# A decoder layer on eight cores: the start of the kernel rearranged, and three reorderings in its second pass

## The chip, the cores and the metric

One Trainium2 chip, eight cores, each with TensorE (PE in the profile), VectorE (DVE), ScalarE (ACT), GpSimd (POOL) and the queue engine SyncE (SP). Every core runs the same program on its own prompt sequence of 2048 rows and its own 16 sample rows, with the same weights. No core waits for another. The metric is the device time of the slowest core in microseconds.

## The reference, cut to what matters

```python
def layer(h, p, prev_a, prev_ffn, ...):
    xn = rmsnorm(h, g_mix)
    z = xn @ w_in                      # 1024 x 7168: x_a, b_a, c_a, u|v, g_a, g_b
    a_conv, new_a = causal_dwconv(c_a * x_a, w_conv_a, prev_a)
    y_a = (b_a * a_conv) @ w_out_a
    u, v = split(gelu(uv)); v = rmsnorm(v, g_v)
    s = chunk_spatial(v, w_spatial, b_spatial)
    y_b = (u * s) @ w_out_b
    m = sigmoid(ga) * y_a + sigmoid(gb) * y_b
    h = h + m @ w_o
    up = rmsnorm(h, g_ffn) @ w_up      # 1024 x 5632
    up_c, new_ffn = causal_dwconv(up, w_conv_ffn, prev_ffn)
    h = h + (gelu(fa) * fb) @ w_down   # 2816 x 1024
    gate = sigmoid(rmsnorm(h, g_ple) @ w_ple_gate)
    return h + gate * (p @ w_ple), ...
```

All inputs and outputs are float32 in memory. The layer runs once for the prompt and once for the sample rows, with a last rmsnorm on both. The weights are used by both groups.

## The kernel before, in words

The 2048 prompt rows go through the layer in two passes of 1024 rows (`pss` 0 and 1), eight tiles of 128 rows each. The 16 sample rows ride along in the second pass (`samp`), as columns 1024 to 1039 of the transposed activations. All products are bfloat16 with sums in PSUM, which has eight banks of 512 float32 columns.

*Order of work.* Every operation is recorded in one list for each engine, in the order of the Python program. `P.op` and `P.dma` derive the semaphore waits from the names that an operation reads and writes, such as `("h", t)` for a tile of rows or `("ps", b)` for a PSUM bank. An engine works through its list strictly in order. So an instruction that waits holds up all behind it on its engine, SP's and POOL's DMA issues among them.

*Weights.* They are packed in memory in the order of their use. `Ring` loads them through POOL's queue, which also casts them to bfloat16, into a ring of eight slots. An item of 512 columns (`w512`) takes two slots and 2 MB of float32, one of 256 columns a slot and 1 MB. `R.limit` caps how many items may have been issued. It is 1 at first (the first value weights, item 0), 2 after the square of row tile 5 (the second value weights, item 1), and open behind the last square.

*The head.* SP issues the loads of the row tiles h0 and h1, then h2 when h0 is there, h3 when item 0 is there, h4 when h1 and item 0 are there, and h5, h6, h7 when h2, h3, h4 are there. A `TileNorm` then takes ACT for the sum of squares, POOL for the inverse root, DVE for the scaling into bfloat16 (L510), PE for eight transposes (L326), and DVE for the copy out of PSUM with the gain (L335). The loop over t runs the value product `B_mm(0, 0, t)` (eight matmuls of 512 columns, L322), `heads[t + 3].scale()` and `heads[t + 2].tp()`. The second half `B_mm(0, 1, t)` needs item 1. PSUM banks 0 to 5 go round among the products, 6 and 7 among the transposes.

*The stages of a pass.* Value product and short conv with its products x, c, b; the spatial gating with the matrix `WsT` and for the sample rows `Ds`, made by `setup_spatial` at j = 4 of the first pass; merge; output product with `w_o` into bank pairs `2 * (t % 3)`, after which DVE adds to h; up product and conv, with `cp` over 11 pairs of weight items; down product; per-layer embedding. In the first `cp` the list `order` says in which order half products ("a" and "b", of blocks q), transposes of the last two row tiles ("T6", "T7"), sample products ("S0", "S1") and the conv of a pair ("E0", "E1") are issued. In the second pass the up products use three bank pairs in rotation, from pair 0, and the transposes and sample products banks 6 and 7. In the down product, four row tiles at a time (`grp`) sum over three weight items (`q`). The sample rows' share `pHs`, in bank 2, follows the four tiles of `grp` 1 after each item.

Of the kernel before, what the change touches and what calls it, by code (L numbers as in the profile page):

```python
# [10 lines left out]
ALU = mybir.AluOpType  # L11
# [3 lines left out]
NS = 16  # L15
# [185 lines left out]
def build_program():  # L201
# [24 lines left out]
    with es:  # L226
# [107 lines left out]
        def TTT(eng, out, in0, in1, op, reads, writes):  # L334
            P.op(eng, lambda e: e.tensor_tensor(out=out, in0=in0, in1=in1, op=op), reads=reads, writes=writes)  # L335
# [20 lines left out]
        class Ring:  # L356
# [8 lines left out]
            def _try_load(self):  # L365
                i = self.next_load
                if i >= NIT or i >= self.limit:
                    return False
                kind, w, k0, nk, c0 = all_items[i]
                ns = 2 if kind == "w512" else 1  # L370
                s = self.slot_ptr
                if ns == 2 and s % 2 == 1:
                    s = (s + 1) % 8
                for q in range(ns):
                    occ = self.occupant[(s + q) % 8]
                    if occ is not None and occ not in self.released:
                        return False
                width = ITEM_W[kind]
                flat = ring[:, s:s + ns, :].rearrange("p a b -> p (a b)")
                land = flat[:, 0:nk * width]  # L380
                dst = land.rearrange("p (k n) -> p k n", k=nk)
                o = ITEM_OFF[i % len(ITEMS)]
                wsrc = wpk_d[o:o + 128 * nk * width].rearrange("(p l) -> p l", p=128)
                res = [("ring", (s + q) % 8) for q in range(ns)]
                P.dma("pool", (lambda e: e.dma_start(out=land, in_=wsrc)), f"wr{s}", writes=res)  # L385
                for q in range(ns):
                    self.occupant[(s + q) % 8] = i
                self.item_slot[i] = (dst, res)
                self.slot_ptr = (s + ns) % 8
                self.next_load += 1  # L390
                return True
# [37 lines left out]
        P.op("pool", lambda e: e.memset(epsc[:, 0:1], EPS), writes=["epsc"])  # L429
        P.op("pool", lambda e: e.memset(epsc[:, 1:2], 4.0 * EPS), writes=["epsc"])  # L430
        R.prefetch()
        v0r = R.item_slot[0][1]
        for t, after in ((2, [("h", 0)]), (3, v0r), (4, [("h", 1)] + v0r), (5, [("h", 2)]), (6, [("h", 3)]), (7, [("h", 4)])):
            load_h(0, t, after)
        P.op("pool", lambda e: e.memset(ones[:], 1.0 / 1024.0), writes=["ones"])
        P.op("pool", lambda e: e.memset(carry_a[:], 0.0), writes=[("carry_a", j) for j in range(8)])
# [19 lines left out]

        def setup_spatial(stg):
            (ws, wsr), (tr, trr) = stg
            TTT("dve", WsT[:], ws[:, 0:1024].rearrange("p (j t) -> p j t", j=8), bc_mid(tr[:, 0:128], 8), ALU.mult, [wsr, trr], ["WsT"])
            for j in range(8):  # L460
                P.op("dve", lambda e, j=j: e.tensor_scalar_mul(out=Ds[:, j, :], in0=idf[0:16, 0:16], scalar1=w00[0:16, j:j + 1]),
                     reads=["cst"], writes=["Ds"])
            wideR.free(wsr)
            wideR.free(trr)
# [151 lines left out]
        for t in range(8):  # L616
            jk, jkr = wideR.get()
            heads.append(TileNorm(h[:, t, :], ("h", t), 128, t * 128, t, 0, dma=False, junk=(jk[:, 0:512].bitcast(BF16), jkr)))
            heads[t].sq()
            if t == 5:  # L620
                R.limit = 2
                R.prefetch()
        R.limit = NIT
        R.prefetch()
        heads[0].scale()
        heads[1].scale()
        heads[0].tp()
        heads[1].tp()
        heads[2].scale()
        for t in range(8):  # L630
            B_mm(0, 0, t)
# [10 lines left out]
        for pss in range(2):  # L642
# [128 lines left out]
                hsf = hs[:].rearrange("p k s -> p (k s)")  # L771
            for t in range(8):
                mres = [("m", k, bi) for bi, (c0, n) in enumerate(blocks) if c0 < (t + 1) * 128 and c0 + n > t * 128 for k in range(8)]
                pO, pOr = psR.at(2 * (t % 3), 2)
                for half in range(2):
                    _, wv_, wvr = wo[half]
                    for k in range(8):
# [74 lines left out]
            for cp in range(11):  # L852
# [1 line left out]
                ib_, wb, wbr = next_item()  # L854
                pairs = {}
                if cp == 0 and samp:
                    order = [(0, "a", 0), "T6", (0, "b", 0), (1, "a", 0), "T7", "S0", "S1", (0, "a", 1), (0, "b", 1), "E0",
                             (1, "a", 1), (1, "b", 0), (1, "b", 1), "E1"]
                elif cp == 0:
                    order = [(0, "a", 0), "T6", (0, "b", 0), (1, "a", 0), "T7", (1, "b", 0), (0, "a", 1), (0, "b", 1), "E0",  # L860
                             (1, "a", 1), (1, "b", 1), "E1"]
                else:
                    order = [(0, "a", 0), (0, "a", 1), (0, "b", 0), (0, "b", 1), "E0", (1, "a", 0), (1, "a", 1), (1, "b", 0), (1, "b", 1), "E1"]
                    if samp:
                        order[5:5] = ["S0"]
                        order.append("S1")
# [43 lines left out]
            if samp:  # L910
                store(cf_d[:, :], carry_f[:].rearrange("p r c -> p (r c)"), "stcf", [("carry_f", c) for c in range(44)])
                store(cfs_d[:, :], sfT[:].rearrange("p s r c -> p (s r c)"), "stcfs", ["sfT"] + [("sfTo", c) for c in range(44)])
            for half in range(2):
                its = [next_item() for _ in range(3)]
                hc = slice(half * 512, (half + 1) * 512)
                for grp in range(2):
# [3 lines left out]
                    for q in range(3):  # L920
                        _, wv_, wvr = its[q]
                        lo, hi = q * 8, min(22, q * 8 + 8)
                        for tt in range(4):
                            t = grp * 4 + tt
                            pp, ppr = bk[tt]
                            for c in range(lo, hi):
                                MM(pp, act[:, c, t * 128:(t + 1) * 128], wv_[:, c - lo, :], c == 0, c == 21,
                                   wvr + [("act", c)], ppr + (["R1busy"] if c == 21 else []), c == hi - 1)
                            if q == 2:
                                STT(h[:, t, hc], pp, 2.0, h[:, t, hc], ALU.mult, ALU.add, ppr + [("h", t)], [("h", t)])  # L930
                                if half == 1:
                                    pipe.push(TileNorm(h[:, t, :], ("h", t), 128, t * 128, t, 2))
                        if samp and grp == 1:
                            for i in range(4):
                                for c in range(lo, hi):
                                    MM(pHs[:, i * NS:(i + 1) * NS], wv_[:, c - lo, i * 128:(i + 1) * 128], act[:, c, 1024:1040],
                                       i == 0 and c == 0, i == 3 and c == 21, wvr + [("act", "s")],
                                       pHsr + (["R1busy"] if c == 21 else []), c == hi - 1)
                            if q == 2:
                                hh = hsf[:, half * 64:(half + 1) * 64]  # L940
                                STT(hh, pHs[:, 0:64], 2.0, hh, ALU.mult, ALU.add, pHsr + ["hs"], ["hs"])
                        if pss == 0 and half == 0:
                            if (grp, q) == (0, 2):
                                sqp = sample_sq()
# [233 lines left out]
```

How the kernel before makes its waits and increments, by code:

```python
            def body(engine, ops=ops):  # L157
                for fn, waits, sig in ops:
                    for k, v in waits:
                        engine.wait_ge(sems[k], v)
                    if fn is None:
                        continue
                    ins = fn(engine)
                    if sig is not None:
                        if sig[0] == "eng":
                            ins.then_inc(sems[sig[1]], 1)
                        else:
                            ins.then_inc(sems[sig[1]], 16)
```

## Time and profile before

| | us |
|---|---|
| median of three runs | 1170.34 (1170.22 to 1171.02) |
| profiled execution, its own time | 1170.05 |
| its span on the slowest core (core 2) | 1168.3 |
| spans of the eight cores | 1163.5 to 1168.3 |
| PE busy (core 2) | 1124.1 (96%) |
| DVE, ACT, POOL busy | 609.8, 384.7, 341.8 |
| chain that ended last, share of PE | 88% |

The span is the time from the first to the last instruction of a core; the profiled execution's own time is 1.75 us longer. All rows below are of core 2 unless they say otherwise. Times in them are microseconds from the start of the span. The granted clock is 1.00 for the higher of PE's two levels. The five DMAs of rows 4 were issued at 1.85 (V0, item 0), 7.6 (h2), 16.4 (h3), 24.4 (h7) and 28.1 (V1, item 1).

### The profile page before, as it was taken

The numbers are of one execution on the slowest core, as the hardware profiler recorded it, in microseconds if no ns is written. First come the engines' busy times: TensorE is split into PE (matmuls) and PEld (weight loads), VectorE is DVE, ScalarE is ACT, GpSimd is POOL, SyncE is SP. The second block draws the span as 40 slices with busy tenths as digits, with TensorE's granted clock in tenths as the row PEclk, the third lists the DMA queues.
The fourth block names the chain that finished last, engine by engine and source line by source line (L and its number), as shares of the span: only waits on it lengthen the run. The fifth ranks groups of instructions, "written<-read, shape, count | busy, mean of one in ns | idle before, by whom it ended". The sixth has DMA issues, their size and how long they took to land.

```text
span 1168.3 us, 18289 instructions; the slowest of 8 cores (1163.5 to 1168.3 us)
## 1 busy us (share of the span) xinstructions
PE 1124.1 (96%) x6425; PEld 574.5 (49%) x6520; DVE 609.8 (52%) x668; ACT 384.7 (33%) x649; POOL 341.8 (29%) x451
## 2 busy tenths in 40 slices
PE   4999999999999999999899999999999999999996
PEld 2444454444444444443446666666644444444443
DVE  3267662123687776124615866322267888871247
ACT  3622221111354444014772223112133444430134
POOL 2411113222234434114832010222223333330144
PEclk9999999999999999999999999999999999999998
DMA  7983642544844333358699355244377343343443
GB/s 185 183 158 72 111 71 46 80 83 78 145 93 72 73 73 72 62 92 192 196 195 233 63 116 90 37 73 73 72 127 127 73 73 73 73 90 64 79 102 129
DMA packets 58585, 119.77 MB, mean 103 GB/s; under 512 B 33264, under 2 KB 34032, under 8 KB 55936
## 3 DMA queue, kind: packets, MB, share of 16 engines
q0 software_dynamic: 20112, 82.85, 40.9%
q1 hardware_dynamic: 38240, 35.58, 11.3%
q8 instruction: 54, 0.88, 0.3%
q14 instruction: 35, 0.29, 0.1%
q10 hardware_dynamic: 144, 0.17, 0.1%
HBM read 184.14 MB, written 9.95 MB: 166 GB/s over the span
## 4 chain that ended last, share of the span: by engine, by line
PE 88%; POOL 3%; issue 2%; DVE 2%; DMA 2%; ACT 1%; DVEq 0%; POOLq 0%; ACTq 0%; SPq 0%
PE pq L322 88%; POOL s_wd L335 2%; DMA s_ring<-wpk 1%; DVE s_wd L338 1%; ACT s_xnb L329 1%; POOL s_st_r L335 1%; POOL s_st_ss L335 1%; DMA s_h<-x 1%; ACT s_wd L329 0%; DVE s_h L338 0%; PE pq L326 0%; POOL s_R L335 0%; DVE s_xnb L510 0%; DVE s_xnb L338 0%; DVE s_xn L335 0%
## 5 line engine op out<-in xcount | busy, mean ns | idle before, releaser
L322 PE MATMUL pq<-s_xn,s_ring 128*128 128x512 bf16 (+3 forms) x3693 | 658.1, 334 | 4.2 <-DVE s_wd L338 0.8
L322 PEld LDWEIGHTS pq<-s_xn,s_ring 128*128 128x128 bf16 x3744 | 335.6, 98 | 313.2 <-issue 2.0
L338 DVE SCALAR_TENSOR_TENSOR s_wd<-pq,s_cst,s_wd 128x1023 f32<-128x1023 f32 (+1 forms) x176 | 225.2, 1282 | 63.1 <-ACT s_carry_f L332 53.8
L335 POOL TENSOR_TENSOR s_R<-s_wd 128x1024 bf16<-128x1024 f32 (+3 forms) x84 | 146.3, 1742 | 357.9 <-DVE s_wd L338 166.6
L322 PE MATMUL pq<-s_ring,s_R 128*128 128x512 bf16 x936 | 206.9, 379 | 2.7 <-DVE s_wd L338 1.4
L338 DVE SCALAR_TENSOR_TENSOR s_wd<-s_wd,pq 128x512 f32<-128x512 f32 (+4 forms) x98 | 66.7, 681 | 193.2 <-PE pq L322 170.4
L329 ACT ACTIVATE s_wd<-pq 128x512 f32<-128x512 f32 (+4 forms) x138 | 78.4, 568 | 240.1 <-PE pq L322 238.7
L329 ACT ACTIVATE s_wd<-pq,s_cst 128x1024 f32<-128x1024 f32 x88 | 98.1, 1114 | 165.5 <-PE pq L322 165.5
L322 PEld LDWEIGHTS pq<-s_ring,s_R 128*128 128x128 bf16 x960 | 93.2, 98 | 112.5 <-issue 1.8
L322 PE MATMUL pq<-s_R,s_ring 128*128 128x347 bf16 (+3 forms) x875 | 125.1, 292 | 0.3
L322 PE MATMUL pq<-s_ring,s_xn 128*128 128x512 bf16 (+1 forms) x514 | 119.6, 383 | 5.3 <-DMA s_ring<-wpk 3.3
L385 POOL DMA_DIRECT2D s_ring<-wpk x134 | 75.0, 564 | 132.7 <-PE pq L322 127.5
L322 PEld LDWEIGHTS pq<-s_R,s_ring 128*128 128x128 bf16 x880 | 69.7, 97 | 50.9
L329 ACT ACTIVATE s_xnb<-s_h 128x1024 bf16<-128x1024 f32 x32 | 33.8, 1057 | 184.8 <-DVE s_h L338 184.4
L322 PEld LDWEIGHTS pq<-s_ring,s_xn 128*128 128x128 bf16 (+1 forms) x528 | 50.4, 98 | 65.2 <-issue 9.8
L335 POOL TENSOR_TENSOR s_st_ss<-s_st_ss,s_epsc 128x1 f32<-128x1 f32 (+1 forms) x81 | 24.3, 300 | 160.3 <-ACT s_xnb L329 139.7
L338 DVE SCALAR_TENSOR_TENSOR s_h<-pq,s_h 128x512 f32<-128x512 f32 x32 | 22.1, 690 | 93.3 <-PE pq L322 93.3
L335 DVE TENSOR_TENSOR s_wd<-pq,s_wd 128x512 f32<-128x512 f32 (+2 forms) x40 | 23.5, 587 | 70.7 <-POOL s_wd L342 26.7
L338 DVE SCALAR_TENSOR_TENSOR s_wd<-s_wd,s_cst 128x1024 f32<-128x1024 f32 x32 | 41.1, 1285 | 24.1 <-ACT s_wd L329 22.5
L335 POOL TENSOR_TENSOR s_st_r<-s_st_ss,s_mhalf 128x1 f32<-128x1 f32 (+1 forms) x81 | 47.3, 584 | 12.0 <-POOL s_st_ss L335 0.9
L329 ACT ACTIVATE s_wd<-s_wd 128x1024 f32<-128x1024 f32 (+1 forms) x45 | 47.3, 1056 | 5.1 <-DVE s_wd L335 5.1
L338 DVE SCALAR_TENSOR_TENSOR s_xnb<-s_h,s_st_r,s_gbc 128x1024 bf16<-128x1024 f32 x28 | 35.9, 1282 | 11.1 <-POOL s_st_r L335 8.5
(81 smaller groups left out, 483.6 us busy)
## 6 DMA issues: line engine op xcount, KB each, us to landing
s_ring<-wpk POOLq DMA_DIRECT2D x110, 512.0 KB, 8.9
s_ring<-wpk POOLq DMA_DIRECT2D x20, 1024.0 KB, 10.0
s_h<-x SPq DMA_DIRECT2D x16, 512.0 KB, 16.1
y<-s_wd SPq DMA_DIRECT2D x15, 512.0 KB, 2.7
s_R<-x SPq DMA_DIRECT2D x8, 512.0 KB, 9.2
s_ring<-wpk POOLq DMA_DIRECT2D x4, 768.0 KB, 7.2
s_gbc<-g_v SPq DMA_DIRECT2D x2, 512.0 KB, 15.0
s_gbc<-g_ffn SPq DMA_DIRECT2D x2, 512.0 KB, 6.3
```

The lines of the kernel that those rows point to most:

```text
L322: P.op("pe", lambda e: e.matmul(out, lhsT=lhsT, rhs=rhs, start=start, stop=stop), reads=reads, writes=writes, signal=signal)
L329: P.op("act", lambda e: e.activation(out=out, in_=in_, func=func, **kw), reads=reads, writes=writes)
L335: P.op(eng, lambda e: e.tensor_tensor(out=out, in0=in0, in1=in1, op=op), reads=reads, writes=writes)
L338: P.op("dve", lambda e: e.scalar_tensor_tensor(out=out, in0=in0, scalar=scalar, in1=in1, op0=op0, op1=op1), reads=reads, writes=writes)
L385: P.dma("pool", (lambda e: e.dma_start(out=land, in_=wsrc)), f"wr{s}", writes=res)
```

## The change

The head: item 0 is loaded by two DMAs, each with half of its columns in memory. The first writes the name `v0a`, the second the ring slots. The products of item 0 wait for both. h2 is released by `v0a`, h3 by h1 and `v0a`, and h4 to h7 by the tile two before each. `R.limit` becomes 2 after the square of tile 4 instead of 5. `warm(18)` and `warm(28)` put products of 128 columns, whose results nobody reads, behind the first and the second transpose, in bank 5. `setup_spatial` moves from DVE to POOL.

The second pass: the bank pairs of the output product start with pair 2. S1 moves behind E0 and the half product (1, "a", 1). The sample rows' share of the down product, now in `sample_H`, comes ahead of the four tiles for the last weight item and not behind them, and with it the update of `hs`.

```diff
@@ Ring._try_load
-                P.dma("pool", (lambda e: e.dma_start(out=land, in_=wsrc)), f"wr{s}", writes=res)
+                if i == 0:
+
+                    for q, wr in ((0, ["v0a"]), (1, res)):
+                        P.dma("pool", (lambda e, q=q: e.dma_start(out=land[:, q * 2048:(q + 1) * 2048], in_=wsrc[:, q * 2048:(q + 1) * 2048])),
+                              "wv0a" if q == 0 else f"wr{s}", writes=wr)
+                else:
+                    P.dma("pool", (lambda e: e.dma_start(out=land, in_=wsrc)), f"wr{s}", writes=res)
...
-                self.item_slot[i] = (dst, res)
+                self.item_slot[i] = (dst, res + ["v0a"] if i == 0 else res)
@@ head
-        v0r = R.item_slot[0][1]
-        for t, after in ((2, [("h", 0)]), (3, v0r), (4, [("h", 1)] + v0r), (5, [("h", 2)]), (6, [("h", 3)]), (7, [("h", 4)])):
+        for t, after in ((2, ["v0a"]), (3, [("h", 1), "v0a"]), (4, [("h", 2)]), (5, [("h", 3)]), (6, [("h", 4)]), (7, [("h", 5)])):
             load_h(0, t, after)
@@ setup_spatial
-            TTT("dve", WsT[:], ws[:, 0:1024].rearrange("p (j t) -> p j t", j=8), bc_mid(tr[:, 0:128], 8), ALU.mult, [wsr, trr], ["WsT"])
+            TTT("pool", WsT[:], ws[:, 0:1024].rearrange("p (j t) -> p j t", j=8), bc_mid(tr[:, 0:128], 8), ALU.mult, [wsr, trr], ["WsT"])
             for j in range(8):
-                P.op("dve", lambda e, j=j: e.tensor_scalar_mul(out=Ds[:, j, :], in0=idf[0:16, 0:16], scalar1=w00[0:16, j:j + 1]),
+                P.op("pool", lambda e, j=j: e.tensor_scalar_mul(out=Ds[:, j, :], in0=idf[0:16, 0:16], scalar1=w00[0:16, j:j + 1]),
@@ head
-            if t == 5:
+            if t == 4:
                 R.limit = 2
                 R.prefetch()
...
+        def warm(n):
+            pw, pwr = psR.at(5)
+            for q in range(n):
+                MM(pw[:, 0:128], ones[:], idb[:], True, True, ["ones", "idb"], pwr, q == n - 1)
+
         heads[0].tp()
+        warm(18)
         heads[1].tp()
+        warm(28)
@@ output product
-                pO, pOr = psR.at(2 * (t % 3), 2)
+                pO, pOr = psR.at(2 * ((t + (2 if samp else 0)) % 3), 2)
@@ up product
-                    order = [(0, "a", 0), "T6", (0, "b", 0), (1, "a", 0), "T7", "S0", "S1", (0, "a", 1), (0, "b", 1), "E0",
-                             (1, "a", 1), (1, "b", 0), (1, "b", 1), "E1"]
+                    order = [(0, "a", 0), "T6", (0, "b", 0), (1, "a", 0), "T7", "S0", (0, "a", 1), (0, "b", 1), "E0",
+                             (1, "a", 1), "S1", (1, "b", 0), (1, "b", 1), "E1"]
@@ down product
+            def sample_H(pHs, pHsr, wv_, wvr, lo, hi, half):
+                for i in range(4):
+                    for c in range(lo, hi):
+                        MM(pHs[:, i * NS:(i + 1) * NS], wv_[:, c - lo, i * 128:(i + 1) * 128], act[:, c, 1024:1040],
+                           i == 0 and c == 0, i == 3 and c == 21, wvr + [("act", "s")],
+                           pHsr + (["R1busy"] if c == 21 else []), c == hi - 1)
+                if hi == 22:
+                    hh = hsf[:, half * 64:(half + 1) * 64]
+                    STT(hh, pHs[:, 0:64], 2.0, hh, ALU.mult, ALU.add, pHsr + ["hs"], ["hs"])
...
+                        if samp and grp == 1 and q == 2:
+                            sample_H(pHs, pHsr, wv_, wvr, lo, hi, half)
                         for tt in range(4):
...
+                        if samp and grp == 1 and q < 2:
+                            sample_H(pHs, pHsr, wv_, wvr, lo, hi, half)
```

## Rows read from the trace of the kernel before

**Rows 1.** Spans and granted clock of all cores.

```profile
core 1: 1163.5 us, clock 0.998
```

**Rows 2.** PE's waits over the span: total, times, longest (us).

```profile
PE pq L326 <- DVE s_xnb L510: 13.6, 5, 10.8
```

**Rows 3.** Timeline of the head: start, length, engine, line, operation, count, idle before.

```profile
16.57 3.57 PE L322 MATMUL pq<-s_ring,s_xn 128*128 128x512 bf16 x8 [3.12 <-DMA s_ring<-wpk]
...
20.21 1.01 PE L326 MATMUL pq<-s_idb,s_xnb 128*128 128x128 bf16 x8
...
24.39 1.06 ACT L329 ACTIVATE s_wd<-s_h 128x1024 bf16<-128x1024 f32 x1 [1.95 <-DMA s_h<-x]
...
25.69 1.06 ACT L329 ACTIVATE s_wd<-s_h 128x1024 bf16<-128x1024 f32 x1
...
28.12 0.59 POOL L385 DMA_DIRECT2D s_ring<-wpk  x1
...
28.71 1.89 PE L322 MATMUL pq<-s_ring,s_xn 128*128 128x512 bf16 x8 [0.53 <-DVE s_xn L335]
...
33.05 1.89 PE L322 MATMUL pq<-s_ring,s_xn 128*128 128x512 bf16 x7
...
39.05 6.20 PE L322 MATMUL pq<-s_ring,s_xn 128*128 128x512 bf16 x27 [0.18 <-DMA s_ring<-wpk]
```

**Rows 4.** DMA issues (V0, h2, h3, h7, V1), last column us to landing.

```profile
s_ring<-wpk POOLq DMA_DIRECT2D x1, 1024.0 KB, 14.5
...
s_h<-x SPq DMA_DIRECT2D x1, 512.0 KB, 9.4
...
s_h<-x SPq DMA_DIRECT2D x1, 512.0 KB, 4.8
...
s_h<-x SPq DMA_DIRECT2D x1, 512.0 KB, 5.1
...
s_ring<-wpk POOLq DMA_DIRECT2D x1, 1024.0 KB, 10.7
```

**Rows 5.** Timeline of core 1 at the end of the first half.

```profile
32.58 7.74 PE L322 MATMUL pq<-s_ring,s_xn 128*128 128x512 bf16 x35
```

**Rows 6.** Stretches of the head: busy by engine, PE clock, DMA share, GB/s.

```profile
9.00:11.00 2.00, 0.16 (x2) 0.19 (x3) 0.75 (x1) 0.97 (x2) 1.43 (x4) 1.00 0.90 139
...
11.00:13.00 2.00, 1.41 (x14) 1.17 (x13) 1.46 (x2) 0.00 (x0) 0.43 (x1) 1.00 1.06 164
...
13.00:15.00 2.00, 0.45 (x5) 0.18 (x2) 1.65 (x2) 0.00 (x0) 0.00 (x0) 1.00 0.91 209
...
15.00:17.00 2.00, 0.43 (x2) 0.18 (x3) 0.00 (x0) 0.00 (x0) 0.00 (x0) 1.00 0.42 164
...
19.00:21.00 2.00, 1.93 (x11) 0.97 (x10) 0.75 (x1) 0.00 (x0) 0.21 (x1) 1.00 1.12 301
```

**Rows 7.** Timeline of DVE in the first conv stage.

```profile
110.01 1.22 DVE L335 TENSOR_TENSOR s_WsT<-s_wd 128x1024 bf16<-128x1024 f32 x1
```

**Rows 8.** Timeline of the second pass, output products to first up products.

```profile
844.82 6.85 PE L322 MATMUL pq<-s_ring,s_R 128*128 128x512 bf16 x31 [0.98 <-DVE s_wd L338]
...
874.04 1.89 PE L322 MATMUL pq<-s_xn,s_ring 128*128 128x512 bf16 x8
...
874.38 1.22 DVE L338 SCALAR_TENSOR_TENSOR s_h<-s_h,pq 128x1024 f32<-128x1024 f32 x1 [1.04 <-PE pq L322]
...
876.42 0.61 PE L326 MATMUL pq<-s_idb,s_xnb 128*128 128x128 bf16 x8 [0.48 <-DVE s_xnb L510]
...
888.54 11.79 PE L322 MATMUL pq<-s_xn,s_ring 128*128 128x512 bf16 x67 [0.80 <-DVE s_wd L338]
```

**Rows 9.** Timeline at the end of the second pass's down stage.

```profile
1118.62 0.75 PE L322 MATMUL pq<-s_R,s_ring 128*128 128x16 bf16 x24
...
1122.41 1.06 ACT L329 ACTIVATE s_xnb<-s_h 128x1024 bf16<-128x1024 f32 x1 [1.06 <-DVE s_h L338]
...
1124.15 1.02 PE L322 MATMUL pq<-s_ring,s_pT 128*128 128x512 bf16 x4 [1.31 <-DVE s_hs L338]
```

More of the change, by code:

```diff
@@ L932, in build_program @@
                                     pipe.push(TileNorm(h[:, t, :], ("h", t), 128, t * 128, t, 2))
[L933 to L941, printed above, removed]
+                        if samp and grp == 1 and q < 2:
+                            sample_H(pHs, pHsr, wv_, wvr, lo, hi, half)
                         if pss == 0 and half == 0:
```

## The prediction

> **What bounds the kernel now.** I first read the spans of all cores [rows 1]. The metric is the slowest core, core 2 with its 1168.3 us of the table above; the reader is to see that core 1 does the same work in 1163.5 us. The profiled execution took 1170.05 us, so 1.75 us lie outside its span, and it is 0.3 us under the median of 1170.34; I add all changes to the median. The table gives TensorE (PE) 1124.1 of 1168.3 us, so about 44 us are not PE, and only these, not the products, can be won by an edit that reorders. The waits of PE [rows 2] say where: the largest entry is the transposes of the head, which wait for scaled rows, 13.6 us in five times, one of them 10.8 us, which is the wait for the first row tile itself. So the second view is the timeline of the first 40 us [rows 3]. Call the eight row tiles of pass 0 h0 to h7, the two loads of value weights V0 and V1, and the eight products of each value half B0 to B7. B0 starts at 16.57, when V0 has landed; B3 at 28.71; B5 at 33.05; the second half starts at 39.05, and from there PE runs without a long gap. The head is therefore worth 39.05 minus 16 products, whatever PE could do.
>
> Three rows tell what B3 waited for. The square of h4 starts at 24.39, when h4 has landed, and B3 starts 4.3 us later. The code says why it is h4 and not h3: the scaling of h(t+1) stands on VectorE (DVE) ahead of the copy that B(t) reads. The transpose of h2 starts at 20.21, and h2 landed at 7.6 + 9.4 = 17.0 [rows 4], 3.2 us before. From B3 on the step is (33.05 - 28.71) / 2 = 2.17 us, PE's own (eight products, eight transposes), and from B5 to the second half it is 6.0 us, of which 0.2 is a wait for V1. So on core 2 three things end within a fifth of a microsecond: the chain h4, B3, four steps; and V1, issued at 28.12 with 10.7 us to landing. Core 1 shows the same program when neither is late [rows 5]: its B6 starts at 32.58 and runs on into the second half without a gap, so that half starts at 36.05. Core 2 is 3.0 us later there, two thirds of the distance of the spans. A head that only helps core 1 is worth nothing to the metric.
>
> **The head, step by step.** (1) *V0 in halves.* The products still name both halves, so B0 starts no sooner by it; the first half is only the token that releases h2 and h3. When does it land? From 9 to 17 us the queues moved 2 x (139 + 164 + 209 + 164) = 1352 thousand bytes [rows 6]; h2 is 524 of them, so V0 took 828 and had 221 of its 1049 before 9.0. Half of V0 is 524, 303 more, and the 139 GB/s of the first row are V0 nearly alone: 2.2 us, so about 11.2. Bounds: 10.3 if the half is served ahead of the tail of h1, 12.5 with one more microsecond of completion. The cost of the second issue on POOL (GpSimd) is one more DMA instruction before two memsets that nobody waits for: nothing.
>
> (2) *h2 and h3.* Before, h2 was issued at 7.6 and took 9.4 us, against 4.8 for h3 [rows 4]: it landed behind V0. Now it is issued at 11.3. The bytes ahead of it are the same and the queues stay busy, so I take 17.0 again; the lower bound is 11.3 + 4.8 = 16.1, the upper one 18. h3 is issued with it and not at 16.4. Four tiles from h3 (21.2) to h7 (24.4 + 5.1 = 29.5) took 8.3 us, 2.1 each, so h3 lands at 19.1 instead of 21.2.
>
> (3) *h4 to h7.* Each is now released by the tile two before it. At 4.8 us a load: h4 17.1 + 4.8 = 21.9, h5 24.0, h6 26.8, and h7 24.1 + 5.1 = 29.2. The new list keeps two loads under way and no more, so the gain shrinks: 2.4 us at h4, 0.3 at h7.
>
> (4) *Fillers.* 18 and 28 products of 128 columns stand behind the two first transposes. B0 took 3.57 us for eight products, 0.45 each, where B3's row shows 1.89: 512 columns in 0.43 us are the lower of the clock's two levels, 1.2 GHz, though the clock column of [rows 6] reads 1.00 there; PE had been idle for 3.12 us. With the fillers it is busy up to V0, and I expect B0 at the higher level, 1.7 us shorter. But the next instruction is the transpose of h2, and that cannot start before 17.0 + 3.2 = 20.2, where it starts now. So the 1.7 us become a wait: worth nothing, unless h2 is sooner. Their cost: 46 products at half of a transposed block's time or so (8 take 1.01 us at the lower level in the row of the transpose) end by about 17.5 at most, up to 0.9 us after V0; hidden by the same wait.
>
> (5) *The chain.* B2 not before 19.1 + 4.3 = 23.4; B3 21.9 + 4.3 = 26.2; B4 28.4 (B3 plus 2.17; h5 gives 28.3); B5 26.8 + 4.3 = 31.1; B6 29.2 + 4.3 = 33.5, and two products follow, so the half starts at 31.1 + 5.8 = 36.9 to 37.1. Against 39.05 that is 2.1 us. (6) *V1 a tile sooner.* Before, the issue at 28.12 came 2.4 us after the square of h5 had started at 25.69 [rows 3]; now it follows h4: 21.9 + 2.4 = 24.3, landing 24.3 + 10.7 = 35.0, inside the 37.0. It buys nothing of itself, but without it V1 would land at 24.0 + 2.4 + 10.7 = 37.1 and set the end. Bounds of the head: 1.0 us gained if h2 is at 18; 4.4 if loads overlap better (rival one). (7) *The spatial setup on POOL.* DVE loses one operation of 1.22 us [rows 7] and eight of 16 columns; PE has no wait there on core 2, so nothing. POOL gets them, at up to twice DVE's time as my guess (no row here shows it); behind them on POOL stand 2-column copies and weight loads. A load that comes some 4 us later costs nothing as long as PE has no wait for the ring there, and it has none behind the head: nothing too.
>
> **The second pass.** (8) *PSUM banks.* Now the first output product goes to banks 0 and 1, and bank 0 is the last one of the merge: PE waits 0.98 us for DVE (the first of [rows 8]). With the banks rotated it goes to 4 and 5, whose readers are done: 0.95 saved. But the eighth tile then lies in banks 0 and 1, and that is where the first up product is written. DVE reads that tile from 874.38 for 1.22 us, to 875.60. The product starts at 874.04 today; it would start at about 875.75, end 1.72 later at 877.5, and the transpose behind it, which starts at 876.42 today after 0.48 us of waiting, starts 1.1 to 1.3 later. So the rotation gives 0.95 and takes 1.2: plus 0.25 us. Between the bounds 0 (if the wait is hidden in what follows) and 1.66.
>
> (9) *S1 later.* Today both sample products stand before the up product that needs the second transposed tile and waits for its copy anyway; moved, S1 (16 products of 16 columns, 0.5 us by the 0.75 of 24 in [rows 9]) falls into the 0.80 us in front of 888.54. It is hidden before and after: 0, at most 0.1 either way. (10) *Sample product of the down stage first.* At the end of the stage PE waits 1.31 us for DVE's update of the sample rows, in bank 2 [rows 9]. Moved ahead of the last four tiles, the update is done early and this wait goes. What is late next: the sample norm's product behind it needs ScalarE (ACT), which first squares the last tile; that square starts at 1122.41, and the tile comes 0.75 us later than before, because the 24 sample products (0.75 us) now precede it. 1122.41 + 0.75 + 1.25 + 0.31 gives 1124.7, and with 0.15 to PE 1124.9, against 1125.0 today (1124.15 plus four products of 0.215). So 0.15 us are left of 1.31; bounds 0 and 1.3.
>
> **Sum.** Head -2.1, bank rotation +0.25, S1 0, sample product -0.15: -2.0 us, 1168.3.
>
> **Rivals.** *One: the head follows bandwidth, not the two loads.* If a tile lands every 1.75 us (524 thousand bytes at the 301 GB/s of the one stretch of [rows 6] that is h loads alone), with h2 at 16.5, h7 is there at 25.5 and PE's own step decides: transposes of h2 at 19.7 (0.45 us), then five steps of 2.17 us and two of 1.72, the half at about 34.5, V1 just there: -4.4, total 1165.9, and 1164.8 if the sample wait goes too. Against it: h3 alone took 4.8 us. The same sum holds for a bank wait that is hidden. *Two, the other side: V1 breaks into h7.* V1 issued at 24.3 moves its first data at about 27 (an estimate: h3's 4.8 us less 1.75 of its own transfer leave 3 us at most), when h7 (issued 24.1) is half done. h2 next to V0 took 4.6 us more than h3. If h7 suffers as h2 did it lands at 29.2 + 4.6 = 33.8, B6 starts at 38.1, and the half at 41.6: +2.5, total 1173. It decides from 2 us of delay of h7 on. For it: h2's row. Against it: h7 is under way first, and V0 was under way before h2. The Trainium skill, "DMA: Bandwidth & Descriptors", section "Queues, rings and completion order", says that an engine takes turns between queues by whole packets of several descriptors and not row by row; by that h2 waited for V0's packet, which agrees with its 9.4 us, and h7, already begun, would lose nothing to V1, so that the sum stays at -2.0 rather than +2.5. *Three: the first half of V0 lands only with the second,* because both go through one queue at the same time. Then h2 is issued at 16.4 and lands at 21.2, h3 at 23.3, h4 at 26.1, h6 at 31.0: B5 35.3, the half at 41.1: +2.0, total 1172.4. Against it: the order of issue.
>
> **From cases to numbers.** About what a measurement of this kernel can tell from no change is 0.2%, 2.3 us; faster means below 1168.0. The forecast 0.55, its own range 1167.0 to 1169.6; it lies across that bound, 0.22 of it below. Rival one 0.23, all faster. Rival two 0.14, in its mild forms within the bound (0.06), else slower (0.08). Rival three 0.08: slower 0.05, within 0.03. So faster 0.45, same 0.42, slower 0.13. The range from 1165.3 to 1171.9 leaves out the far ends of all three.
>
> **What would show it.** Right: h2's transpose at about 20.2; the square of h4 near 22; V1's issue near 24; the second half at 37 on cores 0, 2, 5 and 7; B0 in 1.9 us with a wait behind it; no wait at the first output product, a new one of 1.7 us before the first up product; the wait for the sample update replaced by one for ACT. Wrong: h4 before 21 (rival one), h7 after 31 (rival two), h2 after 20 (rival three), a late stage that gives the head's gain back.

## The result: slower by 0.7%, because h7 waits for V1

| | before | after |
|---|---|---|
| median on the same chip, us | 1171.02 (5 runs) | 1178.95 (1176.71 to 1179.61, 5 runs) |
| ratio after / before | | 1.0068, 95% interval 1.0055 to 1.0080 |
| profiled execution, its own time | 1170.05 | 1176.71 |
| slowest core, its span | core 2, 1168.3 | core 1, 1174.5 |

The change costs 8 us where 2 were forecast as gain. One of the five executions of the kernel before (1258.06 us) was in the chip's slower state, in which the cores of a die show a lower granted clock; the ratios here and below leave such executions out. The first view is again the list of spans; it answers to [rows 1].

```profile
core 0: 1166.4 us, clock 0.996
core 1: 1174.5 us, clock 0.994
core 2: 1172.9 us, clock 0.993
core 3: 1165.2 us, clock 0.996
```

Six cores stand at 1172.9 to 1174.5 us, and two, 0 and 3, at 1166.4 and 1165.2. Something catches a core or misses it. The chain that ended last, on core 2 of the kernel after, names it (start, length, what):

```profile
1.84 9.59 DMA s_ring<-wpk
...
11.93 5.31 DMA s_h<-x
...
17.30 4.97 DMA s_h<-x
...
22.33 12.47 DMA s_h<-x
```

These are the first half of V0 (it lands at 11.43), then h3, h5 and h7, each issued when the one before in the chain has landed. h7 takes 12.47 us where h3 and h5 take 5. The timeline of core 2 of the kernel after (it answers to [rows 3]) has the rest:

```profile
15.04 1.89 PE L322 MATMUL pq<-s_ring,s_xn 128*128 128x512 bf16 x8 [0.85 <-DMA s_ring<-wpk]
19.27 1.01 PE L326 MATMUL pq<-s_idb,s_xnb 128*128 128x128 bf16 x8 [2.34 <-DVE s_xnb L515]
20.07 3.08 PE L322 MATMUL pq<-s_ring,s_xn 128*128 128x512 bf16 x8
...
21.73 1.02 POOL L391 DMA_DIRECT2D s_ring<-wpk  x1
...
34.88 1.06 ACT L329 ACTIVATE s_wd<-s_h 128x1024 bf16<-128x1024 f32 x1 [9.86 <-DMA s_h<-x]
...
38.23 1.01 PE L326 MATMUL pq<-s_idb,s_xnb 128*128 128x128 bf16 x8 [6.39 <-DVE s_xnb L515]
39.47 19.14 PE L322 MATMUL pq<-s_ring,s_xn 128*128 128x512 bf16 x80 [0.22 <-DVE s_xn L335]
58.44 3.83 PE L322 MATMUL pq<-s_xn,s_ring 128*128 128x512 bf16 x17
```

V1 is issued at 21.73 and h7 0.6 us behind it, at 22.3. The DMA issues of the two (the last column is the time to landing) and the stretches of the head answer to [rows 4] and [rows 6]:

```profile
s_ring<-wpk POOLq DMA_DIRECT2D x1, 1024.0 KB, 12.9
...
s_h<-x SPq DMA_DIRECT2D x1, 512.0 KB, 12.5
```

```profile
31.00:33.00 2.00, 0.85 (x4) 0.19 (x2) 0.00 (x0) 0.00 (x0) 0.00 (x0) 1.00 0.54 86
33.00:35.00 2.00, 0.00 (x0) 0.00 (x0) 0.00 (x0) 0.12 (x1) 0.00 (x0) 1.00 0.03 8
...
37.00:39.00 2.00, 0.77 (x8) 0.78 (x8) 1.78 (x2) 1.94 (x4) 2.00 (x5) 0.50 0.24 16
```

V1 lands at 21.73 + 12.9 = 34.6 and h7 at 34.8, right behind it. PE has finished B5 by 31.85, waits 6.39 us for the last scaled row, and then runs at the lower of its two clock levels for a while (0.50 granted in the row from 37 to 39 us): 80 matmuls of 512 columns take 19.14 us, where 80 x 0.215 is 17.2. The first product of the conv stage, the stage after the head, starts at 58.44; on core 2 before it was 52.86. Of these 5.6 us, 3.45 are the later transpose of h7 (38.23 against 34.78) and 2.1 come behind it, 1.9 of them from the clock. I use the start of the conv stage from here on as the mark of the head.

What the slowest cores differ by is (core 1 after against core 2 before): head 60.19 - 52.86 = +7.3; a wait at the end of pass 0 that core 1 does not have, -1.45 (below); second pass +0.3. Together +6.2, the difference of the spans.

The second pass, on core 1 of the kernel after, answers to [rows 8]:

```profile
849.51 7.07 PE L322 MATMUL pq<-s_ring,s_R 128*128 128x512 bf16 x32
...
879.29 1.22 DVE L338 SCALAR_TENSOR_TENSOR s_h<-s_h,pq 128x1024 f32<-128x1024 f32 x1 [1.04 <-PE pq L322]
...
880.66 1.89 PE L322 MATMUL pq<-s_xn,s_ring 128*128 128x512 bf16 x8 [1.54 <-DVE s_h L338]
882.39 0.61 PE L326 MATMUL pq<-s_idb,s_xnb 128*128 128x128 bf16 x8
```

The wait of 0.98 in front of the output products is gone, and one of 1.54 stands in front of the first up product, for the DVE operation on the eighth tile's banks.

### The profile page after: what moved, and what is told of

Read it like the earlier page. It is cut to its first block, busy times and chain, and to the rows that moved or that the text cites. A ratio compares the mean times of both kernels' runs of the same rounds, so it can differ in the third digit from the quotient of the medians.

```text
span 1174.5 us, 18478 instructions; the slowest of 8 cores (1165.2 to 1174.5 us)
## 1 busy us (share of the span) xinstructions
PE 1132.9 (96%) x6566; PEld 579.2 (49%) x6566; DVE 609.0 (52%) x659; ACT 384.5 (33%) x649; POOL 349.7 (30%) x461
## 4 chain that ended last, share of the span: by engine, by line
PE 90%; DMA 3%; POOL 3%; issue 2%; DVE 1%; ACT 1%; DVEq 0%; POOLq 0%; ACTq 0%; SPq 0%
PE pq L322 90%; DMA s_h<-x 2%; POOL s_wd L335 1%; DMA s_ring<-wpk 1%; DVE s_wd L338 1%; POOL s_st_ss L335 1%; POOL s_st_r L335 1%; ACT s_xnb L329 0%; PE pq L326 0%; DVE s_h L338 0%; ACT s_wd L329 0%; POOL s_rsS L335 0%; DVE s_xnb L515 0%; DVE s_xn L335 0%; DVEq L1129 0%
## 5 line engine op out<-in xcount | busy, mean ns | idle before, releaser
L338 DVE SCALAR_TENSOR_TENSOR s_wd<-pq,s_cst,s_wd 128x1023 f32<-128x1023 f32 (+1 forms) x176 | 225.1, 1282 | 63.6 <-ACT s_carry_f L332 53.5
L322 PE MATMUL pq<-s_R,s_ring 128*128 128x512 bf16 (+3 forms) x880 | 125.2, 292 | 0.0
L322 PEld LDWEIGHTS pq<-s_R,s_ring 128*128 128x128 bf16 x880 | 69.4, 97 | 50.4
L329 ACT ACTIVATE s_xnb<-s_h 128x1024 bf16<-128x1024 f32 x32 | 33.8, 1057 | 184.5 <-DVE s_h L338 184.1
L322 PEld LDWEIGHTS pq<-s_ring,s_xn 128*128 128x128 bf16 (+1 forms) x528 | 50.4, 98 | 61.7 <-issue 5.3
L335 POOL TENSOR_TENSOR s_st_ss<-s_st_ss,s_epsc 128x1 f32<-128x1 f32 (+1 forms) x81 | 23.9, 296 | 165.5 <-ACT s_xnb L329 138.0
L338 DVE SCALAR_TENSOR_TENSOR s_wd<-s_wd,s_cst 128x1024 f32<-128x1024 f32 x32 | 42.2, 1318 | 24.1 <-ACT s_wd L329 22.5
L338 DVE SCALAR_TENSOR_TENSOR s_xnb<-s_h,s_st_r,s_gbc 128x1024 bf16<-128x1024 f32 x28 | 35.9, 1282 | 11.2 <-POOL s_st_r L335 7.7
## 6 DMA issues: line engine op xcount, KB each, us to landing
s_h<-x SPq DMA_DIRECT2D x16, 512.0 KB, 17.3
```

The lines of the kernel that those rows point to most:

```text
L322: P.op("pe", lambda e: e.matmul(out, lhsT=lhsT, rhs=rhs, start=start, stop=stop), reads=reads, writes=writes, signal=signal)
L329: P.op("act", lambda e: e.activation(out=out, in_=in_, func=func, **kw), reads=reads, writes=writes)
L338: P.op("dve", lambda e: e.scalar_tensor_tensor(out=out, in0=in0, scalar=scalar, in1=in1, op0=op0, op1=op1), reads=reads, writes=writes)
```

## The experiments

The ratio is against the kernel before on the same chip. "Head" is the range over the eight cores of the start of the conv stage, "h7" that of its square; before they are 49.7 to 53.0 and 26.4 to 29.6, after 50.4 to 60.2 and 28.3 to 37.1.

| experiment | ratio, 95% interval | h7 | head |
|---|---|---|---|
| 1 after, V1 behind h5 again | 1.0018 [1.0009, 1.0027] | 27.6 to 30.6 | 50.8 to 53.2 |
| 2 before, V1 a tile sooner | 0.9994 [0.9985, 1.0003] | 27.6 to 30.6 | 50.3 to 53.5 |
| 3 after, h7 released by h4 | 1.0010 [1.0001, 1.0019] | 25.6 to 29.0 | 50.4 to 53.5 |
| 4 before, second pass of after | 0.9992 [0.9978, 1.0005] | 27.2 to 30.4 | 50.2 to 53.6 |
| 5 before, V1 two tiles sooner | 1.0036 [1.0021, 1.0051] | 27.1 to 32.2 | 50.0 to 54.5 |
| 6 experiment 1 without fillers | 1.0011 [0.9999, 1.0022] | 27.5 to 29.6 | 50.6 to 53.0 |
| 7 before, fillers alone | 1.0005 [0.9996, 1.0014] | 27.5 to 31.0 | 50.4 to 54.9 |
| 8 before, sample product alone | 0.9999 [0.9990, 1.0008] | 27.2 to 29.8 | 50.1 to 54.7 |
| 9 before, h7 released by h6 | 1.0037 [1.0025, 1.0050] | 29.1 to 35.2 | 50.9 to 59.3 |
| 10 after, V1 in two loads | 1.0054 [1.0035, 1.0074] | 27.1 to 38.5 | 49.3 to 62.7 |
| 11 head of 3, no fillers, second pass of before | 0.9987 [0.9975, 0.9999] | 26.8 to 28.4 | 50.2 to 52.0 |
| 12 before, banks alone | none, 1171.16 us once | 27.1 to 30.6 | 50.0 to 54.8 |

**1 and 2: V1's place, alone.** In the kernel after, `if t == 4:` becomes `if t == 5:`; in the kernel before, the reverse.

> The changed kernel, with the one edit that V1 is issued after the square of row tile 5 again. Theory A (V1 reaches the queues at the time of h7, and h7 lands behind it): h7 is back at 5 us from issue to landing on all cores, V1 is issued near 26 and lands near 37, the second half starts at 37 to 38 on the slow cores, and the time is 1168 to 1170 us, ratio 0.998 to 1.000. Theory B (the later release of h4 to h7, each by the tile two before it, costs by itself): h7 still lands after 31 and the time stays above 1175, ratio over 1.004. Theory C (the edits of the second pass cost several us): the head is cured, the time still above 1174.

> The kernel before, with V1 issued after the square of tile 4 instead of 5, and nothing else. In it h7 is released by h4's landing, 2.2 us ahead of V1's issue. Theory A: h7's data are under way first, it lands at 29.5 to 31 on most cores, V1 lands 1.5 to 2 us sooner; the time is 1168 to 1171, ratio 0.998 to 1.001, unless V1 catches h7 on some core, which then shows 10 us and more from issue to landing and about 1175. If issuing V1 a tile sooner is harmful in any order of release: ratio over 1.004.

Putting V1 back takes most of the loss away, though not all of it: the forecast for theory A was a ratio of 0.998 to 1.000, and 1.0018 came out. The rest is looked for below. But V1 sooner in the kernel before costs nothing: there h7 is released by h4 and goes out 2.1 to 2.5 us ahead of V1 on all eight cores. It takes both edits, the earlier V1 and the later h7.

**3: h7 ahead again, V1 early.** In the list of the kernel after:

```diff
-(4, [("h", 2)]), (5, [("h", 3)]), (6, [("h", 4)]), (7, [("h", 5)])
+(4, [("h", 1), "v0a"]), (5, [("h", 2)]), (6, [("h", 3)]), (7, [("h", 4)])
```

> The changed kernel, with the releases of h4 to h7 as before the change, one tile sooner each (h4 by h1 and the first half of V0, h5 by h2, h6 by h3, h7 by h4), V1 still after the square of tile 4. h7 is then issued 2.2 us ahead of V1. Theory A: h4 lands near 20.5, h7 near 27, V1 near 35, the second half starts at 35 to 36.5 on all cores, and the time is 1165 to 1168, ratio 0.995 to 0.998. Theory B says the same of the releases; the two differ in the run without the early V1. If V1 still catches h7: above 1174.

The square of h7 starts by 29.0 at the latest, with V1 left early: the other cure. The time was missed, 1.0010 where 0.995 to 0.998 was expected; the head starts its conv stage at 50.4 to 53.5, not sooner than before.

**5 and 9: the same fault from either side in the kernel before.** Experiment 5 has `if t == 3:`, experiment 9 `(7, [("h", 6)])` with V1 where it was.

> The kernel before with one edit: V1 issued after the square of h3, two tiles sooner (h7 still released by h4, V0 whole, no fillers, second pass unchanged). V1's issue should then stand within about 1 us of h7's on most cores. Theory (a load of h issued less than about 1 us before V1, or behind it, lands only when V1 has landed): the square of h7 moves from 26.4 to 29.6 us to 33 to 37 us on the cores where that happens, the first product of the stage after the head starts near 58 us there instead of 50 to 53, and the time rises by 4 to 8 us (ratio 1.003 to 1.007). Rival (what holds h7 back is two loads in flight and not V1; bandwidth is shared evenly): h7 lands by 31 us on all cores, ratio 0.999 to 1.001.

> The kernel before with one edit: h7 is released by h6 instead of h4. V1 keeps its place behind the square of h5 (issued at 24.6 to 28.2 us); h7 is issued at the landing of h6, 24.8 to 28.4 us, so within about 1 us of V1. Theory (the order of h7 against V1 decides, not that V1 is sooner): h7's square moves from 26.4 to 29.6 us to 35 to 39 us on several cores, where it lands with V1, the stage after the head starts 5 to 9 us later there, and the ratio is 1.003 to 1.008. Rival (an early V1 is harmful because h5 and h6 are still to come, h7's order is not the point): h7 lands 4 to 6 us after its issue, square at 30 to 33 us, stage after the head at most 3 us later, ratio 1.000 to 1.003.

Core 7 of experiment 9, timeline:

```profile
24.87 0.59 POOL L385 DMA_DIRECT2D s_ring<-wpk  x1
25.16 1.06 ACT L329 ACTIVATE s_wd<-s_h 128x1024 bf16<-128x1024 f32 x1 [1.54 <-DMA s_h<-x]
...
35.14 1.06 ACT L329 ACTIVATE s_wd<-s_h 128x1024 bf16<-128x1024 f32 x1 [8.83 <-DMA s_h<-x]
```

h6 lands at 25.1 and sends h7 out 0.3 us behind V1; h7 lands ten microseconds later. V1 was no sooner than in the kernel before, so the rival that blames an early V1 falls: the order of the two counts. This release also delays h7 by itself: on core 4, where it took only 5.6 us, its square starts at 34.1. So the times to landing carry this reading more than the ratio does.

The DMA queues of core 7, from 29 to 31 us and from 31 to 33 (packets, MB, share of the time of the 16 DMA engines), show what goes on meanwhile. q0 carries V1 in 128 packets of 8 KB, q1 carries h7 in 128 packets of 4 KB:

```profile
q0 software_dynamic: 41, 0.34, 80.0%
q1 hardware_dynamic: 44, 0.18, 23.6%
...
q0 software_dynamic: 38, 0.31, 90.5%
q1 hardware_dynamic: 37, 0.15, 20.8%
```

The two take turns, nearly one packet for one, which fits that both land together (34.9 and 35.1), and V1's packets take 80 to 90% of the engines' time. Not every core looks like this. On core 1 of the kernel after, between 26 and 30 us, q0 has 53 packets and q1 a single one, and nearly all of h7 (issued at 24.9) moves after 30. Why it starts so late there no run tells.

In the profiled execution of experiment 5 no core was caught fully (1171.94 us, h7's square by 32.2, where 33 to 37 was expected), but eight of its other eleven executions took 1176 to 1180 us, with single cores some 7 us above the rest. That h7 was caught on these cores is inferred from their times; they have no trace. Read together, the profiled executions of after and of 5, 9 and 10 give 32 cores with h7 from 1.3 us ahead of V1 to 1.6 behind:

| h7's issue against V1's | cores | h7, issue to landing |
|---|---|---|
| ahead by 0.05 to 1.3 us | 19 | 18 in 3.5 to 6.3 us, one 10.7 |
| behind by 0.1 to 1.6 us | 13 | 11 in 8.3 to 12.5 us, two in 5.7 and 7.0 |

In the ten other traces h7 is at least 2.1 us ahead on all 80 cores, and none takes more than 8.2 us.

**10: is it the size of the load?** V1 too goes out as two loads of 512 KB, one behind the other.

```diff
-if i == 0:
+if i < 2:
```

> The kernel after with V1 loaded as two transfers of 512 KB, one issued right behind the other, at the same place. Theory A (a load of h waits for the whole transfer that is ahead of it on the engines, one at a time): h7 is caught by the first half alone and lands 5 to 7 us after its issue; square at 28 to 31 us, ratio 1.001 to 1.003. Theory B (it waits for everything that the other queue has, both halves): h7's square at 33 to 37 us on most cores as in the kernel after, ratio 1.005 to 1.008.

The ratio is theory B's, but neither theory fits all cores. Four have h7 ahead of both halves and land it in 4.2 to 6.2 us. The other four, with h7's issue counted from that of V1's first half:

| core | h7 behind the first half | V1's halves land | h7 lands |
|---|---|---|---|
| 2, ahead of the second half | 0.8 | 32.3 and 36.5 | 32.5 |
| 6, ahead of the second half | 0.4 | 33.3 and 37.2 | 33.6 |
| 3, behind both | 1.3 | 34.8 and 37.5 | 37.3 |
| 5, behind both | 1.6 | 33.8 and 39.0 | 38.4 |

So h7 lands with the load that was issued last ahead of it: with the first half alone on cores 2 and 6, with the second on 3 and 5. That is theory A's rule, but not its size: the half alone still held h7 for 8.3 and 8.9 us, where 5 to 7 were expected.

**6 and 7: the fillers.** The two calls of `warm` are taken out of experiment 1, and put alone into the kernel before.

> The first experiment (the kernel after, V1 again behind the square of h5), and the two groups of filler products taken out. Its only difference from the first experiment, which stood at ratio 1.0018, is the 46 fillers. Theory (the fillers end before the transpose of h2 is due and the clock falls again where B0 waits, so they buy nothing): B0 takes 3.4 to 3.7 us instead of 1.9 and the start of the second half moves by less than 0.5 us, ratio 1.001 to 1.0025. Rival (the fillers pay for part of the head): ratio 1.003 or more, the second half 1 to 2 us later. A third way: they cost something, because the group of 28 holds up the transpose of h2; then ratio 1.000 to 1.001.

> The kernel before with the 18 and 28 filler products alone (V0 whole, the releases and V1 as before, second pass unchanged). Theory (fillers are worth nothing, h2 lands long after them): ratio 0.999 to 1.001, the start of the stage after the head stays at 49.7 to 53.0 us. Rival (full clock at B0 carries through the first half): 1 to 2 us faster, ratio 0.998 to 0.999.

Their worth is nothing that can be measured (1.0011 without them against 1.0018 with them, 1.0005 alone). Core 6 of experiment 6, timeline of PE, shows why the head doesn't gain in another way:

```profile
15.66 3.57 PE L322 MATMUL pq<-s_ring,s_xn 128*128 128x512 bf16 x8 [2.97 <-DMA s_ring<-wpk]
19.82 0.61 PE L326 MATMUL pq<-s_idb,s_xnb 128*128 128x128 bf16 x8 [0.58 <-DVE s_xnb L515]
...
36.77 13.97 PE L322 MATMUL pq<-s_ring,s_xn 128*128 128x512 bf16 x63 [1.10 <-DMA s_ring<-wpk]
```

B0 takes 3.57 us without fillers and still ends before the row of h2 is scaled. With the releases of after and V1 in its old place, the tiles are early enough on this core, and now V1 is what PE waits for, 1.10 us.

**4, 8 and 12: the second pass.** All three edits, the sample product alone, the banks alone. Two stretches are compared on all cores: from PE's last transpose at the head of the second pass (589 us) to that of T6 in the up product, and from there to the end.

> The kernel before, with the three edits of the second pass only: bank pairs of the output product rotated, S1 behind E0, the sample rows' share of the down product ahead of the four tiles. By the intervals of the two profiles (last merge product to the transposes of tile 7 0.14 us longer, down stage to the second gate product 0.40 us shorter) -0.3 us, ratio 0.9995 to 1.0000. Theory C: ratio over 1.003.

> The kernel before with only the sample product moved ahead of the last weight tile's products in the second pass (banks and sample rows as before). With all three edits of the second pass the stretch from the transpose before the down stage to that of T6 was 0.13 us longer and the stretch from T6 to the end 0.3 us longer. Theory: 0.13 is the banks and stays out here (287.7 us), 0.3 is the sample product and stays (292.2 us); ratio 0.999 to 1.001. Rival (0.3 comes of the sample rows' S1, which stands later in the order): 291.9 us here. The prediction had minus 0.15 for this edit, 291.75 us.

> The kernel before with the banks of the merge products rotated in the second pass alone. Theory: the stretch from the last transpose before the down stage to the transpose of T6 is 287.84 us instead of 287.71 on all cores (plus 0.13), the stretch from there to the end stays 291.9. The prediction had plus 0.25 for this edit. Rival (the 0.13 comes of the sample rows): 287.71.

All three edits (experiment 4) make the two stretches 0.13 and 0.3 us longer, where 0.3 less was expected in all; the ratio, 0.9992 with an interval from 0.9978 to 1.0005, cannot tell the two apart. The banks alone: the first stretch is 287.84 on all cores instead of 287.71, +0.13. The sample product alone: 287.71, and the second stretch is 292.15 to 292.24 instead of 291.88 to 291.96, some 0.25 of the 0.3. Of experiments 8 and 12 both theories hold, the rivals do not. Where the 0.25 comes from, on core 1 of experiment 8:

```profile
1119.80 0.29 ACT L329 ACTIVATE s_xnb<-s_hs 128x128 bf16<-128x128 f32 x1
...
1120.35 0.35 PE L322 MATMUL pq<-s_xnb,s_ones 128*128 128x16 bf16 x8 [0.91 <-DVE s_xnb L338]
...
1123.46 0.17 DVE L562 TENSOR_SCALAR s_rsS<-pq 128x16 f32<-128x16 f32 x1
...
1129.85 0.32 PE L322 MATMUL pq<-s_xn,s_ring 128*128 128x16 bf16 x7 [0.51 <-DVE s_xn L335]
```

and on core 1 of the kernel before:

```profile
1119.35 0.31 ACT L329 ACTIVATE s_xnb<-s_hs 128x128 bf16<-128x128 f32 x1 [0.59 <-DVE s_hs L338]
...
1122.32 0.17 DVE L562 TENSOR_SCALAR s_rsS<-pq 128x16 f32<-128x16 f32 x1
...
1129.04 0.35 PE L322 MATMUL pq<-s_xn,s_ring 128*128 128x16 bf16 x8
```

By this point the timeline of core 1 is 0.55 us later in experiment 8 (0.24 in the head, 0.31 between 555 and 590 us). The DVE operation on the sample rows is 1.14 us later, so 0.59 of it the edit's: the last row tile is finished later by about as much, because 24 sample products precede its own, and DVE takes that tile first. The sample products of the gate, six microseconds on, then wait 0.51 us where they had no wait.

**11: the best of it.** The head of experiment 3 without the fillers, the spatial setup on POOL, and the second pass of before.

> A candidate: the head of the experiment with three loads in flight (first half of V0, h4 released with h3, V1 behind the square of h4), without the fillers, and the second pass of the kernel before. The theory (second-pass edits and fillers cost 0.4 us together, the head by itself gains nothing because the square of h7 sooner by 1 to 2 us is met by V1's landing and by the products of the first half): ratio 0.999 to 1.001. Rival (the head gains once the costs are gone): 0.998 to 0.999.

Median 1170.82 against 1171.71 us of the kernel before: better than both kernels, but by 0.13%, less than the bound of the chances. The ratio of 0.9987 lies in the range of the rival (the head gains once the costs are gone), and its interval, 0.9975 to 0.9999, reaches into that of the theory, so the two are not told apart.

**Where the cured heads lose again.** Experiment 1's slowest core, core 5 with a span of 1171.8, starts its conv stage at 52.28, sooner than core 2 before. It loses 3.9 us against that core between the two transposes at 307 and 555 us, at the end of pass 0. The timeline of PE on core 5 there:

```profile
534.08 3.62 PE L322 MATMUL pq<-s_ring,s_xn 128*128 128x512 bf16 x16
542.35 1.86 PE L322 MATMUL pq<-s_ring,s_pT 128*128 128x512 bf16 x4 [4.66 <-DMA s_ring<-wpk]
```

and the load of 512 KB that it waits for, on core 4 (first) and core 5 of the same execution:

```profile
s_ring<-wpk POOLq DMA_DIRECT2D x1, 512.0 KB, 7.2
...
s_ring<-wpk POOLq DMA_DIRECT2D x1, 512.0 KB, 12.4
```

Core 4 starts its conv stage 0.5 us ahead of core 5. That the later core of such a pair loses, and more so when the two are close, is what the 14 traces show taken together, with the cores taken in pairs 0/1, 2/3, 4/5, 6/7 and the loss counted over the shortest stretch, 246.53 us:

| the later core of a pair is behind by | pairs | its loss, median (most) | loss of the earlier one |
|---|---|---|---|
| under 2.35 us | 22 | 1.47 (5.4) | under 0.2 in 16 |
| 2.35 to 5 us | 30 | 0.71 (2.7) | under 0.2 in 28 |
| over 6.5 us | 4 | 0.07 (1.1) | under 0.2 in 2 |

So a late core whose head gets shorter comes closer to its partner and pays some of the gain there. In the kernel after, cores 0 and 1 are 8.4 us apart and neither loses over 0.2. Core 5 of experiment 1, which was 0.6 us better in the head than core 2 before, was 3.3 worse by 555 us. It is a relation over the traces, with bounds chosen from the same 56 pairs, and not shown by an experiment: what the two share was not tried. No kernel that moves the loads at the end of pass 0 was run.

## Why the prediction was wrong

The step that failed is the sixth, "V1 a tile sooner ... It buys nothing of itself", together with its order against step 3. My own numbers had h7 issued at 24.1 and V1 at 24.3: 0.2 us apart, and I took the order as safe. On core 2 h5 landed 2.7 us after h4 (I had 2.1), V1 followed h4's square by 2.1 (I had 2.4), and h7 came out 0.6 us behind V1. Six of eight cores were caught: five with h7 0.5 to 1.1 us behind V1, and core 5 with h7 0.5 us ahead; core 0, with h7 0.5 behind, had it in 5.7 us. This is rival two, to which I gave 0.14. Its row was in the kernel before. [rows 4] have V0 landing at 1.85 + 14.5 = 16.35 and h2, issued 5.7 us behind it, at 17.0; the trace has h2 0.5 to 0.6 us behind V0 on all eight cores. I read that as 4.6 us of extra time. It is a load that lands with the one issued ahead of it, and so read it puts h7 at V1's 35.0.

By the steps of the prediction. (Ahead of them, "39.05 minus 16 products" is a slip: eight products, B0 to B7, stand ahead of the second half. No term uses it.)

1. *V0 in halves*: forecast 11.2, measured 11.43 on core 2, but 11.9 to 13.1 on the others, four of them at or above the upper bound of 12.5. The second half lands 2.5 to 3.3 us later on every core, so rival three falls.
2. *h2 and h3*: 17.0 and 19.1; the squares start at 16.1 to 17.9 and 17.3 to 19.4. Right.
3. *h4 to h7*, forecast of the landing and measured start of the square: h4 21.9 (19.6 to 22.2), h5 24.0 (22.35 to 24.9), h6 26.8 (23.9 to 26.9). The loads landed from 3.0 us sooner to 0.8 us later than forecast; h7 29.2, measured 34.0 to 37.1 on six cores and 29.9 and 28.3 on the two that were missed. That "the gain shrinks" as two loads are kept under way is what made h7 late enough to be caught.
4. *Fillers*: B0 in 1.89 us with a wait of 2.34 behind it, and worth nothing, as said. Not foreseen: around that wait the granted clock falls again (1.00 from 15 to 19 us, 0.52 from 19 to 21), and B1 takes 3.08 us on core 2.
5. *The chain*: -2.1 for the head. Even where h7 is not caught the gain is missing: experiments 1 and 6 have the head at 50.6 to 53.2 against 49.7 to 53.0. The size was wrong because h7 is no sooner than before (27.5 to 30.6 against 26.4 to 29.6), and where the tiles are early enough V1 can set the end (1.10 us of wait, core 6 of experiment 6).
6. *V1*: 0 forecast, measured +5 to +8 on the caught cores (conv stage at 58.3 to 60.2 against 52.5 to 53.0 on the later cores before). Experiment 1 shows that this one line carries 5 to 6 of the 8 us (ratio 1.0018 against 1.0068; medians, from two sets of runs, 1173.79 against 1178.95). Rival two had the place and the point from which it decides (2 us of delay), but at +2.5 a third of the price: h7 stood 4.6 us behind its 29.2 in that sum and is 4.8 to 7.9 behind; and B6 followed its square by 4.6 and not 4.3 us, with PE at the lower clock (1.9 us).
7. *Spatial setup on POOL*: no wait of PE that it would explain. From the conv stage's start to the transpose at 307 us every trace, with it or without, has 254.51 or 254.52.
8. *Banks*: +0.25 forecast, +0.13 measured; the new wait 1.54 where 1.7 was forecast. Right in kind.
9. *S1*: 0 forecast; experiments 12 and 8 give +0.13 and +0.25 of the +0.13 and +0.3 that all three edits cost, so at most 0.05 is left for it.
10. *Sample product*: -0.15 forecast, +0.25 measured. The square of the sample rows was put rightly behind the last tile's, but I stopped at PE's next wait; the one that counts is ten microseconds on, for the same rows.

The argument against rival two was that h7 is under way first. On 18 of 19 cores with h7 ahead this held; on core 5 of the kernel after h7 was 0.5 us ahead and still took 10.7 us. The Trainium skill, "DMA: Bandwidth & Descriptors", section "Queues, rings and completion order", has each DMA engine take turns between queues, a whole packet of several descriptors at a time. That a load already begun loses nothing was my conclusion from it and stands in no sentence of the page. Turns do show on core 7 of experiment 9, but nearly one for one in the trace's packets of one row each, and by them the late load ends with the large one. The measurement decides: a margin of 0.2 us at the issue was no margin.

## What to carry to other kernels

When two edits move two transfers of different queues towards each other, compute the distance of their issues and not only their landings: if the order can turn within the scatter of the cores (here some 2 us), the price is the landing of the big one, on some cores in some executions. Follow a moved result to its last reader, not to the next wait. And a gain at the start of a kernel is measured at its end: here pairs of cores that come closer together lose it again at the end of pass 0.

## What the runs showed of the hardware

- A load of 512 KB on SP's queue, issued 0.1 to 1.6 us behind a load of 1 MB on POOL's, landed within 0.6 us of it on 11 of 13 cores, 8.3 to 12.5 us after its issue instead of 3.5 to 6.3. With the 1 MB split in two (four of the 11) it landed with the half issued last ahead of it.
- While h7 was held on core 7 of experiment 9 the DMA engines were busy, and the two loads took turns (79 packets of V1 and 81 of h7 from 29 to 33 us). On core 2 of the kernel after the queues moved only 8 GB/s from 33 to 35 us, at a share of 0.03, but that is the tail: most of V1 and h7 had moved before, and the landing waited for the last packets.
- The time to landing of the same load differs within pairs of cores: 7.2 and 12.4 us at the end of pass 0.
